# Delta-rule inverse in a decoder trunk: joining the 64-row halves by groups of four heads

## The reference, cut to what matters

```python
kk = jnp.einsum('nbhik,nbhjk->nbhij', k_beta, kc) * seg
a_mat = jnp.eye(L, dtype=F32) + jnp.where(strict, kk, 0.0)
rhs = jnp.concatenate([v_beta, k_beta * jnp.exp(b)[..., None]], axis=-1)
sol = lax.linalg.triangular_solve(a_mat, rhs, left_side=True, lower=True)
...
v_new = u_c - jnp.einsum('bhik,bhkv->bhiv', w_c, S)
o = jnp.einsum('bhik,bhkv->bhiv', q_d, S) + jnp.einsum('bhij,bhjv->bhiv', a_c, v_new)
S = S * jnp.exp(bl)[..., None] + jnp.einsum('bhjk,bhjv->bhkv', k_o, v_new)
```

## Time and profile before

| | us |
|---|---|
| median of 3 runs | 2435.92 |
| the profiled execution, device time | 2436.91 |
| its span (first to last instruction) | 2435.1 |
| TensorE busy | 2303.9 (95%) |
| VectorE busy | 1497.9 (62%) |
| ScalarE busy | 940.9 (39%) |
| GpSimd busy | 870.6 (36%) |

### The profile page before, as it was taken

The page is one execution under the profiler, slowest core; times in us unless marked ns, Lnnn a source line. Parts: engine busy times, 40 slices in busy tenths (PEclk is TensorE's granted clock), DMA queues, the critical chain, the costliest instruction groups (busy, mean ns, idle before and its releaser), DMA issues. The chain is left out here.

```text
span 2435.1 us, 54588 instructions
## 1 busy us (share of the span) xinstructions
PE 2303.9 (95%) x21003; PEld 1623.7 (67%) x21020; DVE 1497.9 (62%) x3167; ACT 940.9 (39%) x2596; POOL 870.6 (36%) x1090
## 2 busy tenths in 40 slices
PE   6999999999799997799999999996999999999997
PEld 2444444444556653588888888786787887878785
DVE  3343647561578765578576784565666676767665
ACT  3544444434111212444443543434444444444431
POOL 1552322323111111122222220116756566665652
PEclk8999999999899999899999999997999999999998
DMA  9453675855464445786766767546523231322213
GB/s 311 136 180 106 211 222 164 240 159 179 145 233 151 157 141 179 240 301 225 217 216 191 217 208 221 164 132 172 149 89 97 71 115 63 100 85 88 80 41 91
DMA packets 372150, 394.99 MB, mean 162 GB/s; under 512 B 39599, under 2 KB 263023, under 8 KB 371938
## 3 DMA queue, kind: packets, MB, share of 16 engines
q1 hardware_dynamic: 337826, 360.28, 47.1%
q10 hardware_dynamic: 34112, 31.71, 4.2%
HBM read 275.19 MB, written 116.72 MB: 161 GB/s over the span
## 5 line engine op out<-in xcount | busy, mean ns | idle before, releaser
L2792 DVE SCALAR_TENSOR_TENSOR inc_acc<-inc_ub,inc_taps,inc_acc 128x512 f32<-128x512 f32 x288 | 245.4, 852 | 11.0 <-ACT inc_acc L2632 4.2
L758 PE MATMUL inab_b<-inab_wt,keep 128*128 128x512 f16 x768 | 166.7, 379 | 1.6 <-POOL inab_wt L575 1.6
L758 PE MATMUL inab_b<-inab_wt,raw_next 128*128 128x512 f16 x768 | 166.4, 379 | 0.0
L2569 POOL COPY inc_halo<-inc_ub 128x3 f32<-128x3 f32 x96 | 49.0, 510 | 315.1 <-DVE inc_ub L2780 180.7
L1390 PE MATMUL mixab_y<-keep,mixab_oT_hi 128*128 128x512 f16 x512 | 153.1, 381 | 7.4 <-DVE mixab_f_y L1470 5.7
L739 POOL TENSOR_TENSOR inab_a_out<-inab_stage,inab_a_out 128x384 f16<-128x384 f32 x64 | 65.8, 1027 | 212.5 <-ACT inab_a_out L730 212.5
L758 PEld LDWEIGHTS inab_b<-inab_wt,keep 128*128 128x128 bf16 (+1 forms) x768 | 75.1, 98 | 91.1 <-issue 1.9
L758 PEld LDWEIGHTS inab_b<-inab_wt,raw_next 128*128 128x128 bf16 (+1 forms) x768 | 75.1, 98 | 89.9
L2636 ACT ACTIVATE inc_acc<-inc_acc 128x512 f32<-128x512 f32 x96 | 60.5, 630 | 141.6 <-DVE inc_acc L2792 141.4
L3607 DVE STREAM_TRANSPOSE mixc_N<-mixc_T 128x256 f32<-128x256 f32 (+1 forms) x130 | 57.9, 445 | 92.1 <-ACT mixc_T L3432 92.1
L2908 PE MATMUL inc_b<-inc_room,keep 128*128 128x256 bf16 (+3 forms) x864 | 109.3, 279 | 2.7 <-DVE stage_next L2762 2.7
(11 more groups left out here) (625 smaller groups left out, 6058.7 us busy)
## 6 DMA issues: line engine op xcount, KB each, us to landing
keep<-tmp_w SPq DMA_DIRECT2D x336, 256.0 KB, 3.3
tmp_qkv<-inc_acc SPq DMA_DIRECT2D x96, 256.0 KB, 2.8
inab_stage<-in_w_in_c SPq DMA_DIRECT2D x128, 128.0 KB, 2.6
tmp_w<-inab_stage SPq DMA_DIRECT2D x64, 256.0 KB, 3.2
inab_stage<-in_w_in_ab ACTq DMA_DIRECT2D x24, 512.0 KB, 4.1
tmp_w<-inab_a_out SPq DMA_DIRECT2D x64, 192.0 KB, 2.6
stage_next<-in_w_ada ACTq DMA_DIRECT2D x6, 2048.0 KB, 15.1
raw_next<-tmp_qkv SPq DMA_DIRECT2D x8, 1536.0 KB, 6.8
```

The costliest lines, as they stand in the source:

```text
L758: last = nc.tensor.matmul(dst, lhs(a, k), rhs(b, k), start=(k == 0 and i == 0), stop=(k == KT - 1 and i == len(PASSES) - 1))
L2569: pool.tensor_copy(halo[:, g, :], ub[w % 2][side][:, BLK:]).then_inc(halo_saved[side], 1)
L2792: ins = dve.scalar_tensor_tensor(a_v, u_[:, i:i + BLK], taps[:, g, i:i + 1], a_v, ALU.mult, ALU.add)
```

## The change

The two joining products are made group by group, and there are three blocks on TensorE where there were two. `across_first` makes the first product for heads 0 to 3. `across_both`, behind `state_outputs`, makes the first product for heads 4 to 7 and the second product for heads 0 to 3, one of each in turn. `across_last`, behind `turn_o`, makes the second product for heads 4 to 7. The banks change: the first product of group 0 goes to A1 and that of group 1 to A0; the second of group 0 goes to A0 and that of group 1 to A1. The copies of ScalarE and of VectorE are split into two of 64x256 each. `across_first` waits for `attn_ready` of group 1, because bank A1 held the scores of that group. `state_keys` now waits for VectorE's copy of each group, where only its group 1 waited before.

```diff
--- before.py
+++ after.py
@@ -3086,7 +3086,8 @@
     LY = [half_view(x)[:, 0:4] for x in (A0, C0)]
     LT = [half_view(x)[:, 0:4] for x in (B0, C1)]
     LN = [half_view(x)[:, 4:8] for x in (B0, C1)]
-    L64Y, L64N = half_view(A0), half_view(A1)
+    L64Y = [half_view(x)[:, 0:4] for x in (A1, A0)]
+    L64N = [half_view(x)[:, 0:4] for x in (A0, A1)]
 
     Ss = ph.sb("Ss", [P, H, NSEQ, DV])
     s = ph.sem
@@ -3447,8 +3448,9 @@
 
         def across(t):
 
-            act.wait_ge(y64_mm, t + 1)
-            act.activation(Y64[HALF[1]], L64Y[HALF[1]], ACT.Copy, scale=-1.0).then_inc(y64_ready, 1)
+            for g in GRP:
+                act.wait_ge(y64_mm, nth(t, g))
+                act.activation(Y64[HALF[1], gs(g), :], L64Y[g][HALF[1]], ACT.Copy, scale=-1.0).then_inc(y64_ready, 1)
 
         def first_outputs(t, n, par):
             for g in GRP:
@@ -3626,8 +3628,9 @@
 
         def across(t):
 
-            dve.wait_ge(n64_mm, t + 1)
-            dve.tensor_copy(N[HALF[0], :, HALF[1]], L64N[HALF[0]]).then_inc(n64_ready, 1)
+            for g in GRP:
+                dve.wait_ge(n64_mm, nth(t, g))
+                dve.tensor_copy(N[HALF[0], gs(g), HALF[1]], L64N[g][HALF[0]]).then_inc(n64_ready, 1)
 
         def corrected(t, par, n, bank):
 
@@ -3913,20 +3916,36 @@
                 beside(k, 1)
             tn_products(t, len(widths) - 1, 1, halves, widths)
 
-        def across_y(t):
+        def y64(h):
+            return mm(L64Y[h // 4][HALF[1], h % 4, :], BT[HALF[0], h, HALF[1]], T[HALF[0], h, :], start=True, stop=True)
+
+        def n64(h):
+            return mm(L64N[h // 4][HALF[0], h % 4, :], Y64[HALF[1], h, :], N[HALF[1], h, HALF[1]], start=True, stop=True)
+
+        def across_first(t):
+
+            pe.wait_ge(attn_ready, nth(t, 1))
+            wait_apart(pe, t_copied, nth(t, 0, NL, NL - 1), fin.tick)
+            for i, h in heads(0):
+                last = y64(h)
+            last.then_inc(y64_mm, 1)
+
+        def across_both(t):
 
             wait_apart(pe, t_copied, nth(t, 1, NL, NL - 1), fin.tick)
-            for h in range(H):
-                last = mm(L64Y[HALF[1], h, :], BT[HALF[0], h, HALF[1]], T[HALF[0], h, :], start=True, stop=True)
-            last.then_inc(y64_mm, 1)
-
-        def across_n(t):
-
-            for g in GRP:
-                inverse_ready(t, g)
-            wait_apart(pe, y64_ready, t + 1, fin.tick)
-            for h in range(H):
-                last = mm(L64N[HALF[0], h, :], Y64[HALF[1], h, :], N[HALF[1], h, HALF[1]], start=True, stop=True)
+            inverse_ready(t, 0)
+            wait_apart(pe, y64_ready, nth(t, 0), fin.tick)
+            for i in range(4):
+                y_last, n_last = y64(4 + i), n64(i)
+            y_last.then_inc(y64_mm, 1)
+            n_last.then_inc(n64_mm, 1)
+
+        def across_last(t):
+
+            inverse_ready(t, 1)
+            wait_apart(pe, y64_ready, nth(t, 1), fin.tick)
+            for i, h in heads(1):
+                last = n64(h)
             last.then_inc(n64_mm, 1)
 
         def state_outputs(t, par):
@@ -3939,8 +3958,7 @@
 
         def state_keys(t, par):
             for g in GRP:
-                if g == 1:
-                    pe.wait_ge(n64_ready, t + 1)
+                pe.wait_ge(n64_ready, nth(t, g))
                 for i, h in heads(g):
                     last = mm(A[g][:, i, :], qkv[par][:, 8 + h, :], S[:, h, :], start=True, stop=True)
                 last.then_inc(r_mm, 1)
@@ -3982,11 +4000,12 @@
 
             levels(t, BOTH, LEVELS, beside)
             turn_k(t + 1, nxt, half, n2, 0)
-            across_y(t)
+            across_first(t)
             state_outputs(t, par)
+            across_both(t)
             if t >= 1:
                 turn_o(t - 1, P)
-            across_n(t)
+            across_last(t)
             state_keys(t, par)
             grams(t + 1, nxt, n2)
             values(t, P)
```

## The result

The changed kernel takes 2442.05 us (median of 15 runs, 2436.08 to 2449.64), against 2437.66 us for the kernel before in runs beside it (15 runs, 2431.53 to 2443.95). The ratio is 1.0023 [1.0013, 1.0032]: about 5.6 us slower by it (the two medians differ by 4.4), where 3.6 us faster was forecast. The profiled execution took 2443.27 us, 6.4 us more than that of before.

A forecast was written before the change was run, and what follows sets the result against it. TensorE's own order was taken to bound the kernel. Tiles 1 to 15 gain 3.8 us (2.55 order, 1.27 stalls), tile 0 loses 0.25: 3.6 us less, 2432.3 us against the 2435.9 median; range 2428.5 to 2438.5.

The forecast's parts named there:

- TensorE's order in a steady tile: First product to state_keys: 0.47 us saved by pairs, 0.29 for a third quarter visit, turn_o's stall gone; 4.83 instead of 5.14.
- Crossed quarters don't overlap: Rival, middle block: pairs take turns at 58 ns per MATMUL, 7.5 us more, 2439.8; at 0.1 us, 2452; chance 0.09.
- The third visit is cheap: Rival, TensorE's added change to quarters: mostly hidden, 0.29 us in 16 tiles comes back, 4.6 us more gain, 2427.7; chance 0.09.
- The stall does not go: Rival, turn_o: its wait for VectorE's gate stays because gate moves too; only 2.3 us gained, 2433.6; chance 0.1.
- I cost all this at nothing: Work behind ScalarE's waiting second copy: queue 1.8 us late, delays on TensorE, GpSimd and VectorE covered, so 0 us.
- the margin of 0.4 us: VectorE's key_products against GpSimd's segw, 1.8 us later: about 0.4 us of cover left, read in tile 6.
- TensorE's wait for it: Tile 0, ahead of the third block: without turn_o TensorE waits 0.72 us for ScalarE's copy; tile 0 loses 0.25 us.
- ScalarE's queue becoming a wait: Rival: the copy or squares behind it come too late; 0.5 us more per tile, 8 us, 2440; chance 0.05.
- Satisfied waits are free: TensorE's additional waits, all for things done by then, cost nothing: passing five takes 0.20 us, as passing one does.
- tile 15's own 0.25 us: Last tile's gain in the sum: 0.17 us from TensorE's shorter order and 0.08 from turn_o's stall behind gate.

The follow-up runs named there:

- two-visit kernel: Changed kernel with ScalarE's second copy behind key_squares, state loads in tile 14, and across_first directly behind the levels, ahead of turn_k: 2433.84 us, 0.9974.
- the late ScalarE: Kernel before, but in tile 0 alone ScalarE waits for state_outputs ahead of key_copy: 2437.82 us, 1.0012.
- the moved code: Changed kernel with 96 more wait and count instructions, once, on TensorE ahead of tile 0: 2441.02 us, 1.0010.
- the squares first: Changed kernel with ScalarE's second copy of the first product behind key_copy of group 1 and key_squares of group 0: 2438.23 us, 1.0016.
- the pairs in turn: Changed kernel, middle block with four first products, then four second products, not alternating: 2444.44 us (5 runs), 1.0040.
- late loads: Kernel before with SyncE's eight state loads moved from tile 0 to tile 14: 2436.16 us, 0.9997.

## Why the prediction was wrong

- *TensorE's order in a steady tile* (0.47 saved, 0.29 for the visit, the stall gone): right. 4.83 us as forecast, pairs 0.46 us, `turn_o` 0.82, and 3.83 us over fourteen tiles, where the sum had 3.57. "Crossed quarters don't overlap" is wrong: a pair steps at 58 ns. "The third visit is cheap" is wrong by the same 4.83 us, and by the two-visit kernel, in which a tile gains when it goes. "The stall does not go" is wrong too: `turn_o` takes 0.82 us in every tile.
- *"I cost all this at nothing"*, of the queue behind ScalarE's waiting copy: this step failed, in tile 0. I took the margin of 0.4 us from tile 6 and let it stand for all 16. VectorE reaches `key_products` 9.73 us behind the first product in tile 6 (1954.13) but 7.40 us in tile 0 (1702.36). GpSimd's `segw` starts at the same distance in both, 6.20 and 6.11 us. Two things of the tile before give tile 6 its 2.3 us, and tile 0 has neither. One is `turn_o` on TensorE: VectorE's copy of the second product starts at 5.25 us in tile 6 and at 4.23 in tile 0. The other is `oT_rest` on VectorE (L3670), ahead of `key_products` in tile 6 of the kernel before; in tile 0 they follow `corrected` at once:

```profile
1952.81 1.40 DVE L3670 SCALAR_TENSOR_TENSOR mixc_oT_lo<-mixc_y,mixc_gn,mixc_oT_hi 128x512 f16<-128x512 f32 x2
```

```profile
1700.28 2.16 DVE L3641 SCALAR_TENSOR_TENSOR mixc_X<-mixc_A,mixc_col,mixc_vtok 128x128 f32<-128x128 f32 x8 [0.41 <-PE mixc_A L3945]
```

The missing `gate` isn't it: in its place VectorE splits weights, 3.15 us where `gate` takes 3.43. A half of `segw` takes 1.02 us, so tile 0 had a margin of 0.3 us (7.40 less 7.13) for a queue 1.9 us late. I had seen that tile 0 has no `turn_o` and priced TensorE's wait for it (0.25 us net; `state_keys` came 0.37 late), but did not ask the same question on VectorE. The rival that I gave 0.05, ScalarE's queue becoming a wait, is what happened, in one tile of sixteen and at a higher price than 0.5 us: 3.3 us at the state products. Of these 0.4 is `corrected` (L3644 and L3641) starting later against the first product, 1.2 the wait, and 1.6 VectorE's longer operations beside GpSimd (1.21 and 0.42).
- *What follows a late start* was not in the sum at all. Of tile 0's 7.3 us, 3.3 are the chain, 1.5 the longer standstill, and 2.4 the clock: the state products and what follows take 5.20 instead of 4.38 us at a granted 0.53 (0.63 before), and the last stretch 13.07 instead of 11.45 at 0.87 where it was 1.00. Borne out by experiments: the chain by the late ScalarE in the kernel before (4.3 us in tile 0, the clock's fall at the state products included), the standstill by the moved code (2.9 us).
- *Satisfied waits are free*: not contradicted in the change's own tiles, which came out as the sum without them, but wrong as a rule, since 6 more instructions a tile cost 0.2 us.
- *The tail* was not in the sum either, apart from tile 15's own 0.25 us, and it is half as large a loss as tile 0's: +3.5 us. What differs is for how long the clock stays at half in it: before,

```profile
2403.91 2.02 PE L4042 MATMUL mixc_A<-mixc_X,mixc_BT 64*128 64x128 f32 x16 [1.04 <-DVE mixc_Ss L3747]
```

and after, behind the same wait,

```profile
2406.79 3.75 PE L4061 MATMUL mixc_A<-mixc_X,mixc_BT 64*128 64x128 f32 x16 [1.04 <-DVE mixc_Ss L3750]
```

Over the end of the tail, from 70 us behind tile 15's first product, the granted clock is 0.81 before and 0.70 after. It comes back in each profile of the same kernel: 107.93 and 108.09 us before, 111.42 and 111.49 after (111.42 with the squares first). But it isn't the work of the change in the tail: with the 96 instructions ahead of tile 0 the changed kernel has 108.05, with the pairs in turn 108.36, and the kernel before with late loads 110.18. What decides where the clock falls stays open.
- *The whole*: tile 0 +7.3, tiles 1 to 14 -3.8 and the tail +3.5 make 7.0 us in this pair of profiles, 6.4 with the start of the phase, against 5.6 by the ratio of 15 runs each. The forecast of -3.6 was missed by the first and the last term, and the first is the one that is explained.
- Open as well is why one piece of the program is late and another is not. That it depends on the load of the DMA engines was shown, and that it depends on the position of the cuts is well supported; the rule behind it was not found.

## What to carry to other kernels

A margin read in a steady tile holds for steady tiles: for a queue that is made late, look up the margin again in the first and last one, on each engine that waits, because work that gave cover there may be missing. An operation that waits longer is better put behind the work in its queue that others need. A wait put to "issue" is worth following on the other engines: of the three in the kernel with the squares first, one was a late piece of the program, one a late load and one VectorE. And a kernel in which TensorE waits somewhere can pay more than the wait: in tile 0 the clock behind it and the longer standstill turned 3.3 us into 7.3.

## What the runs showed of the hardware

- TensorE's program comes in pieces of 16 KB by DMA. With the eight state loads in tiles 0 and 1 it stood still for 0.5 to 4.7 us, in the middle of a block or between two, without a semaphore that explains it. With these loads in tile 14 it was 2.22 and 1.95 us in two profiles, and in three there was no such standstill. In the eleven profiles that have such standstills they end 2.3 to 2.9 us behind the start of a piece of the program, in the changed kernel 2.7 and 2.6 us.
- After such a standstill, and after waits of 4.6 us, the granted clock is at its lower level (1.2 GHz) for some us: 16 MATMULs of 128x128 then take 3.78 us where they take 2.05, and a block of the levels 1.07 where it takes 0.63. Behind the same wait of 1.04 us in the tail 16 MATMULs took 2.02 us in one kernel and 3.75 in another.
- Two operations of VectorE with both inputs in SBUF take 0.76 us nearly alone (0.2 us beside GpSimd's) and 1.68 or 1.97 us beside them. The Trainium skill ("SBUF — State Buffer", Terms) says that the two engines share a port pair, that one instruction holds it to its end and the other blocks; the 1.97 us agree in kind.
- Two blocks in different quarters overlap without being interleaved in the program: 8 and 8 MATMULs take 0.74 us that way, where they take 0.46 in turn. The alternation is worth the 0.28 us between them.
